# Gathering a unit's rows one unit further ahead, between the scatter-adds of the unit before

## What is computed

```python
def grouped_moe(h, w_router, b_router, w_gate, w_up, w_down):
    scores = jax.nn.sigmoid(xt @ w_router)           # 4096 tokens x 32 experts
    ... # best of 4 groups, then the top 2 experts in it; gates normalised
    def expert_block(args):
        xb, e = args
        hb = jax.nn.silu(xb @ w_gate[e]) * (xb @ w_up[e])   # 1024 -> 512
        return hb @ w_down[e]                               # 512 -> 1024
    ...
    contrib = ys[dest] * sorted_gate[:, None]
    out = jax.ops.segment_sum(contrib, sorted_tok, num_segments=T)
```

## Time and profile before

| | before |
|---|---|
| median of 3 runs | 2438.42 us (2435.72 to 2439.93) |
| the profiled execution | 2431.16 us, span 2429.4 us |
| PE busy | 2152.7 us (89%) |
| PE weight loads busy | 1819.1 us (75%) |
| DVE busy | 1373.7 us (57%) |
| ACT busy | 1000.2 us (41%) |
| POOL busy | 580.5 us (24%) |
| DMA queue q1 (SP) | 307.12 MB, 38.6% of 16 engines |
| DMA queue q0 (POOL) | 128.01 MB, 21.4% of 16 engines |
| mean granted TensorE clock | 0.943 of full speed |
| chain that ended last | PE 67%, DMA 19%, issue 6%, POOL 4% |

### The profile page before, as it was taken

One profiled execution on the slowest core, in us unless ns is written; L12 is line 12 of the kernel. 1 busy time (PEld: TensorE's weight loads), 2 busy tenths in 40 slices (PEclk: granted clock), 3 DMA queues, 4 the chain that ended last, 5 costly groups with the idle time before them and its releaser, 6 DMA issues.

```text
span 2429.4 us, 37501 instructions
## 1 busy us (share of the span) xinstructions
PE 2152.7 (89%) x12222; PEld 1819.1 (75%) x12223; DVE 1373.7 (57%) x2253; ACT 1000.2 (41%) x1442; POOL 580.5 (24%) x493
## 2 busy tenths in 40 slices
PE   8999899999998289999999999999999999999600
PEld 3443778878886288998898998899989888989600
DVE  3221258888888546555555555555555555555298
ACT  2221133223332255544545555554554554545243
POOL 1000034444444301111111211112111111121166
PEclk9999999999999589999999999999999999999855
DMA  5980243333433357776776867777677676776386
GB/s 218 288 283 0 81 142 128 123 121 130 143 123 139 121 150 225 200 195 182 209 200 170 240 178 187 223 199 194 185 191 227 177 221 184 193 213 177 74 298 239
DMA packets 136067, 435.59 MB, mean 179 GB/s; under 512 B 30912, under 2 KB 35008, under 8 KB 131904
## 3 DMA queue, kind: packets, MB, share of 16 engines
q1 hardware_dynamic: 98592, 307.12, 38.6%
q0 software_dynamic: 37440, 128.01, 21.4%
HBM read 328.01 MB, written 108.10 MB: 180 GB/s over the span
## 4 chain that ended last, share of the span: by engine, by line
PE 67%; DMA 19%; issue 6%; POOL 4%; DVE 2%; POOLq 1%; ACT 0%; SPq 0%; ACTq 0%; DVEq 0%
PE ps L867 19%; PE ps L749 15%; PE ps L891 12%; DMA sums<-yrow_b,ent_now 6%; DMA sums<-yrow_a,ent_now 6%; DMA xrow_b<-h_rows,ent_in 5%; PE ps L686 5%; POOL fin_r L1655 3%; PE ps L855 3%; DMA sums<-yrow_c,ent_now 3%; PE ps L731 2%; PE ps L705 2%; PE ps L783 2%; PE ps L640 1%; PE ps L899 1%
## 5 line engine op out<-in xcount | busy, mean ns | idle before, releaser
L891 PE MATMUL ps<-wd_hi,hidT 128*128 128x512 f32 x1056 | 302.1, 412 | 0.4 <-ACT hidT L1089 0.4
L1349 DVE TENSOR_TENSOR wd_lo<-wraw,wd_hi 128x1024 fp32r<-128x1024 f32 x132 | 161.8, 1226 | 198.9 <-ACT wd_hi L1047 198.6
L891 PEld LDWEIGHTS ps<-wd_hi,hidT 128*128 128x128 f32 x1056 | 196.8, 195 | 38.3 <-ACT hidT L1089 0.8
L1349 DVE TENSOR_TENSOR wg_lo<-wraw,wg_hi 128x1024 fp32r<-128x1024 f32 x132 | 161.5, 1225 | 92.6 <-ACT wg_hi L1047 92.6
L1349 DVE TENSOR_TENSOR wu_lo<-wraw,wu_hi 128x1024 fp32r<-128x1024 f32 x132 | 160.7, 1218 | 52.3 <-ACT wu_hi L1047 52.2
L867 PE MATMUL ps<-mxT_hi,wg_hi 128*128 128x256 f32 (+1 forms) x1056 | 164.2, 298 | 12.7 <-issue 12.7
L1089 ACT CAST hidT<-hid 128x320 fp32r<-128x320 f32 x132 | 60.6, 459 | 257.3 <-DVE hid L1428 257.3
L867 PEld LDWEIGHTS ps<-mxT_hi,wg_hi 128*128 128x128 f32 x1056 | 150.3, 192 | 17.4 <-issue 15.6
L867 PE MATMUL ps<-mxT_lo,wg_hi 128*128 128x256 f32 (+1 forms) x1056 | 163.1, 297 | 0.0
L867 PE MATMUL ps<-mxT_hi,wg_lo 128*128 128x256 f32 (+1 forms) x1056 | 162.5, 296 | 0.0
L867 PE MATMUL ps<-mxT_hi,wu_lo 128*128 128x256 f32 (+1 forms) x1056 | 161.9, 296 | 0.0
(11 more groups left out here) (210 smaller groups left out, 4106.9 us busy)
## 6 DMA issues: line engine op xcount, KB each, us to landing
wraw<-expert_w_gate SPq DMA_DIRECT2D x132, 512.0 KB, 5.3
wraw<-expert_w_up SPq DMA_DIRECT2D x132, 512.0 KB, 5.6
wraw<-expert_w_down SPq DMA_DIRECT2D x132, 512.0 KB, 3.4
xch<-x SPq DMA_DIRECT2D x16, 1024.0 KB, 6.6
first_stage<-ych SPq DMA_DIRECT2D x16, 1024.0 KB, 8.2
yt<-first_stage SPq DMA_DIRECT2D x16, 1024.0 KB, 4.9
fin_r<-sums SPq DMA_DIRECT2D x32, 512.0 KB, 4.1
out<-fin_r SPq DMA_DIRECT2D x32, 512.0 KB, 2.9
```

The source lines that it names most:

```text
L891: mm = nc.tensor.matmul(psY[h], hidT[:, l, c, t * P:(t + 1) * P], wd[r][:, c, cols], start=(i == c == 0), stop=(i == 2 and c == FC - 1))
L1349: nc.vector.tensor_tensor(piece(1, j), wraw[:, j % SLOTS, :], piece(0, j).bitcast(F32), ALU.subtract).then_inc(wlo_ok, 1)
```

## The change

Three things.

1. POOL gathers two units ahead instead of one. `unit(u)` now does: scatter-add a; await it once the second half of results is there; issue scatter-add b; wait until the rows of u+1 have been transposed; issue the gather of u+2; await b; scatter-add c and await it (if wide); copy `ent_next` to `ent_now`; await the gather of u+2; copy `ent_in` to `ent_next`, raise `ent_ok`. Units 0 and 1 are gathered ahead of the loop. Awaiting a gather stands in a function of its own, `gathered`.
2. The entries go through `ent_in` (u+2), `ent_next` (u+1) and `ent_now` (u), each holding another unit, where `ent_in` and `ent_next` held the same before. SP loads the entries of u+1, not of u, in its pass for unit u, and behind piece 3, not behind piece 1. Its wait `own_wait(sp, ent_ok, u + 1, ...)` is met at the end of POOL's `unit(u - 2)`.
3. The loops of POOL and SP stop earlier, and the last units are written out behind them; for this DVE puts one more number into `utab`.

The diff:

```diff
@@ -266,7 +266,7 @@
-        utab = keep.take("utab", 4 * LANES + 2, I32)[0:1, :]
+        utab = keep.take("utab", 4 * LANES + 3, I32)[0:1, :]
@@ -457,6 +457,9 @@
+        def before_last(eng):
+            return eng.value_load(utab[:, 4 * LANES + 2:4 * LANES + 3], min_val=E - 2, max_val=MAX_UNITS - 2)
+
@@ -576,16 +579,23 @@
             for j in range(SLOTS, PIECES):
                 load_piece(0, 0, j)
             sp.wait_ge(tab_ok, 1)
-            units = sp.value_load(utab[:, 4 * LANES:4 * LANES + 1], min_val=E, max_val=MAX_UNITS)
-            with sp.Fori(1, units) as u:
-                e, row = unit_expert(sp, u), unit_row(sp, u)
+            own_wait(sp, ent_ok, 1, sp_gate)
+            load_entries(unit_row(sp, 1))
+
+            def load_unit(u, more):
+                e = unit_expert(sp, u)
                 for j in range(PIECES):
                     load_piece(u, e, j)
-                    if j == 1:
-
-                        own_wait(sp, ent_ok, u, sp_gate)
+                    if j == 3 and more:
+
+                        row = unit_row(sp, u + 1)
+                        own_wait(sp, ent_ok, u + 1, sp_gate)
                         load_entries(row)
 
+            second_last = before_last(sp)
+            with sp.Fori(1, second_last + 1) as u:
+                load_unit(u, True)
+            load_unit(second_last + 1, False)
             sp.wait_ge(moe_done, 1)
 
             acc_v = acc[0:S, :].rearrange("(t p) d -> p t d", p=P)
@@ -1380,6 +1390,8 @@
             nc.vector.tensor_copy(utab[:, 4 * LANES:4 * LANES + 1], ucum[0:1, E - 1:E])
             nc.vector.tensor_scalar(utab[:, 4 * LANES + 1:4 * LANES + 2], ucum[0:1, E - 1:E], -1.0, None,
                                     ALU.add)
+            nc.vector.tensor_scalar(utab[:, 4 * LANES + 2:4 * LANES + 3], ucum[0:1, E - 1:E], -2.0, None,
+                                    ALU.add)
             dve.wait_ge(utab_ps, 1)
             nc.vector.tensor_tensor_scan(utab[:, 3 * LANES:4 * LANES], psTab[:, 2 * P:2 * P + LANES],
                                          zer[0:1, :], 0.0, ALU.add, ALU.add)
@@ -1609,6 +1621,10 @@
                     pool.indirect_dma_start(
                         xrow[2], None, hd, bass.IndirectOffsetOnAxis(ap=ent_in[0:LANES, 2, 0:1], axis=0)
                     ).then_inc(xcrow_in, 16)
+
+            def gathered(u):
+                wide = unit_wide(pool, u)
+                with pool.If(wide > 0):
                     own_wait(pool, xcrow_in, 16 * wides_to(pool, u), pool_gate)
                 own_wait(pool, xrow_in, 32 * u + 32, pool_gate)
 
@@ -1616,35 +1632,53 @@
                 pool.indirect_dma_start(acc, bass.IndirectOffsetOnAxis(ap=ent_now[0:n, t, 0:1], axis=0),
                                         yrow[t], None, compute_op=ALU.add).then_inc(done, 16)
 
-            def unit(u, more):
+            def turned(u):
+                pool.wait_ge(x_ps, 4 * u + 4)
+                own_wait(pool, xc_ps, u + 1, pool_gate)
+
+            def unit(u, ahead):
                 wide = unit_wide(pool, u)
-                if more:
-                    pool.wait_ge(x_ps, 4 * u + 4)
-                    pool.wait_ge(xc_ps, u + 1)
-                    gather(u + 1)
-                    gather_c(u + 1)
-                    nc.gpsimd.tensor_copy(ent_next, ent_in).then_inc(ent_ok, 1)
                 for t in range(2):
                     pool.wait_ge(ya_ok, 2 * u + t + 3)
                     own_wait(pool, yd_ok, 2 * u + t + 3, pool_gate)
+                    if t:
+                        own_wait(pool, y_out, 32 * u + 16, pool_gate)
                     scatter(t, P, y_out)
-                    own_wait(pool, y_out, 32 * u + 16 * t + 16, pool_gate)
+                if ahead == 2:
+                    turned(u + 1)
+                    gather(u + 2)
+                    gather_c(u + 2)
+                own_wait(pool, y_out, 32 * u + 32, pool_gate)
                 with pool.If(wide > 0):
                     own_wait(pool, yc_ok, 2 * u + 4, pool_gate)
                     scatter(2, LANES, yc_out)
                     own_wait(pool, yc_out, 16 * wides_to(pool, u), pool_gate)
-                if more:
-                    own_wait(pool, ent_ok, u + 2, pool_gate)
+                if ahead:
                     nc.gpsimd.tensor_copy(ent_now, ent_next).then_inc(entc_ok, 1)
                     own_wait(pool, entc_ok, u + 2, pool_gate)
+                if ahead == 2:
+                    gathered(u + 2)
+                    nc.gpsimd.tensor_copy(ent_next, ent_in).then_inc(ent_ok, 1)
+                    own_wait(pool, ent_ok, u + 3, pool_gate)
 
             gather(0)
             pool.wait_ge(tab_ok, 1)
             gather_c(0)
+            gathered(0)
             nc.gpsimd.tensor_copy(ent_now, ent_in).then_inc(ent_ok, 1)
             own_wait(pool, ent_ok, 1, entc_ok)
             pool.sem_inc(ya_ok, 2)
-            all_units(pool, unit)
+            turned(0)
+            gather(1)
+            gather_c(1)
+            gathered(1)
+            nc.gpsimd.tensor_copy(ent_next, ent_in).then_inc(ent_ok, 1)
+            own_wait(pool, ent_ok, 2, pool_gate)
+            second_last = before_last(pool)
+            with pool.Fori(0, second_last) as u:
+                unit(u, 2)
+            unit(second_last, 1)
+            unit(second_last + 1, 0)
             pool.sem_inc(moe_done, 1)
 
 
```

## The result

The changed kernel takes 2351.67 us (median of 4 runs, 2350.37 to 2351.83) against 2437.07 us before (4 runs, 2434.33 to 2439.93): a ratio of 0.9648, 95% interval 0.9632 to 0.9665, 3.5% faster.

A forecast was written before the change was run, and what follows sets the result against it. PE bounds the kernel, stalling in 16 expert units for gathered rows behind POOL's serial chain. 80.4 - 7 (SP's wait) - 0.4 (small things) = 73 us off 2438.4 gives 2365 us, range 2353 to 2413.

The forecast's parts named there:

- The ceiling: Expert units: the excess of 16 stalled units over their unstalled periods, 80.4 us, the most any gather change can gain.
- The gather's step: POOL: gathers go out 2.4 us after scatter-add b and land 12.0 (two) or 14.5 us (three) after b's issue.
- The middle between the nearest rows on both sides: Gather landing behind b: 12.0 and 14.5 us taken, between 10.4 and 13.0 (own times) and 17.1 and 19.7.
- the upper end: Gather landing if b and the gathers run strictly one after the other: 17.1 (two) or 19.7 us (three) after b's issue.
- the residue of 7 us: SP's new wait behind piece 3 delays weight pieces 4 to 11; loss in narrow units, 7 us in all.
- threshold: Narrow units: weight piece 4 may come at +28.5 us after PE's first product before PE notices.
- slope: Beyond ACT's slack, each further us of lateness of the weights costs PE 12 to 15 us over the kernel.
- B: SP's wait bites partly: pieces land 2.5 us later than taken, residue 35 us, 2393 to 2408 us; chance 0.20.
- the 6 us between profile and median: Gain subtracted from the runs' median, 2438.4 us, not the profiled execution's 2431.16, from which 2358.2 would follow.
- The range: Whole kernel: forecast time between 2353 and 2413 us.
- C: Rows still late: gathers share engines with scatter-add b, 1 to 2 us stalls before wide units, 2388 us; chance 0.06.
- D: Scatter-add b, gathers and c strictly in sequence, late piece 4 behind SP's wait: 61 us slower, 2500 us; chance 0.14.

The follow-up runs named there:

- wait_behind_7: Changed kernel with SP's wait and the entry loads behind piece 7 instead of piece 3: 2351.6 us, ratio 0.9657.
- order_only: Changed kernel with SP's side as before the change, keeping only POOL's new order: 2351.8 us, ratio 0.9652.
- entries_twice: Changed kernel with each unit's four entry DMAs issued twice, the second time into an unread buffer, making SP 3.0 us later: 2376.34 us, ratio 0.9741.
- lag2: Changed kernel with two idle POOL operations per unit between the gather's landing and SP's release: 2416.75 us, ratio 0.9891.
- order_behind_b: Changed kernel with SP's side as before the change and the gather issued behind the landing of scatter-add b, not its issue: 2373.08 us, ratio 0.9714.
- old_place: Changed kernel keeping buffers, early entries and SP's late wait, but with the gather back behind b, c and the copy: 2418.13 us, ratio 0.9896.
- lag1: Changed kernel with one idle POOL operation per unit between the gather's landing and SP's release: 2372.71 us, ratio 0.972.

## Why the forecast missed, step by step

**The ceiling** (80.4 us) held within 1.3 us: the profiled execution of after has its losses down by 86.3 - 4.6 = 81.7 us and its time by 2431.16 - 2350.37 = 80.8 us. The slow clock behind long stalls, counted in the sum, came back with them.

**The gather's step** held: issued 2 us behind b, landed 9.7 to 12.7 us after it (two gathers, median 11.7) and 12.7 to 15.5 (three, median 13.9), where I took 12.0 and 14.5, rows in time in every unit but the first. The 4.0 us from which I took the price of two copies hold only one, at 1562.21; that estimate of 0.8 us was 0.3. The middle between the nearest rows on both sides was the right choice; the upper end (strict sequence, 17.1 and 19.7) did not occur. The Trainium skill (DMA: Bandwidth & Descriptors, Queues, rings and completion order) says, of the queues of SP and ACT, that descriptors are consumed in ring order, but also that a later one may finish its write before an earlier one. So my step from it, that the gathers cannot pass b, was stronger than the page. The trace of POOL's queue agrees with the order as a tendency: b kept its 8.3 us, the gathers took the delay, and of 78 gathers issued within 7 us behind b one landed before it, by 0.07 us.

**The term that failed first is the residue of 7 us** for SP's wait; it is 0, as the runs `wait_behind_7` and `order_only` show. Its place and its threshold were right, and its slope as long as the clock stays up. What was mis-sized is when piece 4 is there. I had the release too late: SP's first entry load went out at +19.5 to +19.9, not +20.7, in narrow units before wide ones behind a narrow one, and at +16.9 to +19.0, not +19.6, in those behind a wide one. I had put two copies behind the last gather (1.2 us), but behind a narrow unit the one to `ent_now` is made while the gather is still in flight (1158.49 and 1162.25 in the timeline of POOL), so that 0.5 us are left; and behind a wide unit c landed in 6.5 us on the median and not 8.5. And I had the landing of piece 4 too long, some 4.3 instead of 5.6 us, since I took a median from a busy time for a moment at which my own mechanism had emptied the queue. It was cast at +26.8 to +27.2 where I had it landing at +29.3: at least 1.3 us inside the slack instead of 0.8 outside. I had even written down that the engines are emptier while SP waits, as an argument against B, and not used it in the sum.

**The second is the 6 us between profile and median.** I added them as if they belonged to every kernel. They were stalls in the main: the first profile fell on an execution with 86 us of losses, the second, 8 us slower, on one with 96, and when the stalls go, so does the difference. The 42 runs of the kernel before taken here and with the experiments reach from 2424 to 2452 us, the four of after from 2350.4 to 2351.8. But scatter does not go with the stalls altogether: the four runs of `order_only`, in which PE does not stall either, reach from 2346.4 to 2354.2. Made against its own time, the sum without the residue gives 2431.2 - 80.4 - 0.4 = 2350.4, which is what the profiled execution of after took; that it agrees to a tenth is luck, since the losses fell by 81.7 and not by 80.4. 7 + 6 = 13 us make up the miss of 13.7 us within the scatter.

**The range** was wrong on its lower side for the same reason: 2353 was median less ceiling less a few microseconds, while the ceiling had been measured on the execution with the smaller losses.

**The rivals.** B's mechanism is real (`entries_twice`, `lag2`), with a feedback that I had missed and that makes it steeper. C's late rows are real in `order_behind_b`, once the gathers wait for b's landing. D's sign was wrong: even with its order made by hand the kernel stays 0.8% faster than before (interval 0.5 to 1.1%), since c and the gathers land faster with the weights held back. That effect also makes `old_place` faster than the kernel before, which no theory of mine had.

Not tried: what makes the stalls of the kernel before longer in one execution than in another, and how the 64 us or so of gain that are not due to the overlap with b divide between c and the copy.

## What to carry to other kernels

When one queue's wait moves back behind another's work, do the sum in absolute times (when does the transfer land, when is it wanted), take the landing from the traffic that the change leaves and not from today's median, and follow the consumer's order one step on: a late operand may delay the very release it waits for. A gain that removes stalls also removes the scatter that came from them, so put the sum on the profiled execution and compare the losses of two profiles before adding an offset. And undo each half: here the reordering of one engine gives all of the gain, and the earlier loading of the entries only adds a wait that must be hidden. For a slack of PE, price also the lower clock: the same lateness cost 2.6 us in one unit and 4 in others.

## What was not expected of the hardware

A queue that is held back speeds the other one: in `old_place`, with SP's weights waiting, the 512 KB scatter-add b landed in 6.5 instead of 8.2 us and the 256 KB one c in 5.5 instead of 7.6. Scatter-add a landed no faster.

A POOL operation that reads and writes SBUF can stop a VectorE one. In `lag1` the idle multiply and a weight split started 0.06 us apart (timelines of POOL and DVE):

```profile
1170.50 1.89 POOL L1664 TENSOR_TENSOR lag<-lag 128x1024 f32<-128x1024 f32 x1 [4.43 <-DMA xrow_c<-h_rows,ent_in]
...
1170.56 2.91 DVE L1361 TENSOR_TENSOR wg_lo<-wraw,wg_hi 128x1024 fp32r<-128x1024 f32 x1 [0.46 <-ACT wg_hi L1059]
```

The split takes 1.23 us elsewhere and 2.91 here, as if it had stood still for most of the 1.89 us. So a probe made of POOL arithmetic is not a neutral delay beside VectorE work.

The other way around, a VectorE operation can hold a POOL one, and this happens in the kernel after itself (timelines of POOL and DVE):

```profile
1287.52 1.27 POOL L1661 COPY ent_next<-ent_in 128x6 int32<-128x6 int32 x1 [1.07 <-issue]
...
1287.52 1.23 DVE L1359 TENSOR_TENSOR wg_lo<-wraw,wg_hi 128x1024 fp32r<-128x1024 f32 x1 [0.46 <-ACT wg_hi L1057]
```

The copy of six columns takes 0.19 us elsewhere and 1.27 here. In this execution 18 copies of entries take 0.35 us or more, and each of them begins while a VectorE operation that reads two SBUF tensors is under way and ends 0.05 us after it. The copy to `ent_next` is what releases SP. In `entries_twice` five of the six narrow units before wide ones therefore have SP's entry loads at the same +21.2, though their copies begin anywhere from +19.9 to +20.7.
